# One-hot products for the last two experts, and a final LayerNorm that reads PSUM

## The reference

```
ffn = moe_ffn(x)                 # top 6 of 64 experts per token, each row weighted, summed per token,
                                 # plus one shared expert
x   = layer_norm(ALPHA * x + ffn, ln2_g, ln2_b)
```

## Time and profile before

| | |
|---|---|
| median of 3 runs | 1415.52 us (1412.44 to 1415.74) |
| the profiled execution's own time | 1414.83 us |
| its span, first to last instruction | 1412.7 us |
| last matmul ends (expert 63, down) | 1372.6 us |
| last scatter lands | 1381.7 us |
| last VectorE instruction ends | 1408.4 us |

### The profile page before, as it was taken

One profiled execution on the slowest core, in us unless ns is written; L12 is line 12 of the kernel. 1 busy time (PEld: TensorE's weight loads), 2 busy tenths in 40 slices (PEclk: granted clock), 3 DMA queues, 4 the chain that ended last, 5 costly groups with the idle time before them and its releaser, 6 DMA issues.

```text
span 1412.7 us, 23233 instructions
## 1 busy us (share of the span) xinstructions
PE 1287.0 (91%) x8205; PEld 743.2 (53%) x8206; DVE 447.3 (32%) x893; ACT 309.6 (22%) x825; POOL 283.4 (20%) x356
## 2 busy tenths in 40 slices
PE   8999999999999997999999999968797999988980
PEld 6465565556555445888846854534343444534430
DVE  1545544544441543333234711101111211111106
ACT  2232331333131343222223111101111011111110
POOL 2201110110110332000000132332223132342132
PEclk8999999999999998999999999988998999998995
DMA  4541111112300112333682189999999999999984
GB/s 123 165 126 39 45 52 52 52 45 81 119 1 0 45 45 68 90 93 85 232 349 87 42 325 392 396 387 401 401 408 390 407 388 375 371 382 395 405 294 182
DMA packets 126441, 294.35 MB, mean 208 GB/s; under 512 B 13008, under 2 KB 82768, under 8 KB 101664
## 3 DMA queue, kind: packets, MB, share of 16 engines
q1 hardware_dynamic: 108592, 265.66, 49.4%
q0 software_dynamic: 15632, 25.47, 7.6%
q10 hardware_dynamic: 2144, 2.22, 0.5%
HBM read 278.83 MB, written 27.04 MB: 217 GB/s over the span
## 4 chain that ended last, share of the span: by engine, by line
PE 34%; DMA 22%; DVE 3%; issue 1%; SPq 0%; ACT 0%; POOLq 0%; POOL 0%; DVEq 0%; ACTq 0%
DMA expert_gu<-in_expert_w_gate_up_dram 14%; PE bank L1227 11%; PE bank L1795 10%; PE bank L1802 5%; PE bank L1233 4%; DMA expert_down<-in_expert_w_down_dram 4%; DMA sum_rows<-expert_y,row_col 2%; PE bank L1787 1%; PE bank L1867 1%; DMA sum_rows<-over_y,over_row_col 1%; PE bank L1255 1%; PE bank L1846 1%; PE bank L1248 0%; DVE x_rows L2007 0%; DVE x_rows L2014 0%
## 5 line engine op out<-in xcount | busy, mean ns | idle before, releaser
L1795 PE MATMUL bank<-expert_gu,gathered_xT 128*64 128x256 f32 x2048 | 263.1, 411 | 52.5 <-DMA expert_gu<-in_expert_w_gate_up_dram 51.4
L442 PE MATMUL bank<-xT,w_head 128*128 128x512 f32 x480 | 241.0, 613 | 1.2 <-PEq L85 1.2
L1795 PEld LDWEIGHTS bank<-expert_gu,gathered_xT 128*64 128x64 f32 x2048 | 147.9, 142 | 148.8 <-DMA expert_gu<-in_expert_w_gate_up_dram 43.5
L1957 DVE SCALAR_TENSOR_TENSOR hidden<-gate,slot_w,bank 128x128 f32<-128x128 f32 x64 | 22.2, 347 | 436.4 <-ACT gate L1919 430.9
L1802 PE MATMUL bank<-expert_down,hiddenT 128*64 128x512 f32 x512 | 123.7, 603 | 1.6 <-issue 0.8
L1697 POOL DMA_INDIRECT sum_rows<-expert_y,row_col x64 | 101.2, 1581 | 49.4 <-POOL row_col L1692 47.9
L442 PEld LDWEIGHTS bank<-xT,w_head 128*128 128x128 f32 x480 | 78.8, 190 | 48.6 <-issue 42.5
L620 POOL TENSOR_TENSOR LO<-LT_diagonal,level_blocks 128x256 f32<-128x256 f32 x48 | 38.2, 830 | 233.5 <-DVE LT_corner L786 233.5
L1919 ACT ACTIVATE gate<-bank 128x128 f32<-128x128 f32 x64 | 17.8, 278 | 301.6 <-PE bank L1795 298.4
L1930 ACT COPY expert_y<-bank 128x512 f32<-128x512 f32 x63 | 36.9, 586 | 130.2 <-PE bank L1802 130.2
L1692 POOL COPY row_col<-row_idx 128x1 int32 (+1 forms) x64 | 12.5, 196 | 261.6 <-ACT expert_y L1930 166.7
(11 more groups left out here) (331 smaller groups left out, 1856.8 us busy)
## 6 DMA issues: line engine op xcount, KB each, us to landing
expert_gu<-in_expert_w_gate_up_dram SPq DMA_DIRECT2D x128, 1024.0 KB
expert_down<-in_expert_w_down_dram SPq DMA_DIRECT2D x64, 1024.0 KB
w_head<-in_w_in_dram SPq DMA_DIRECT2D x32, 512.0 KB, 3.9
w_tile<-in_w_in_dram SPq DMA_DIRECT2D x15, 512.0 KB, 4.2
sum_rows<-zero_rows SPq DMA_DIRECT2D x2, 2048.0 KB, 12.1
w_tile<-in_w_branch_a_dram SPq DMA_DIRECT2D x7, 512.0 KB, 5.4
w_pair<-in_w_in_dram SPq DMA_DIRECT2D x6, 512.0 KB, 5.2
x_rows<-in_x_dram SPq DMA_DIRECT2D x4, 512.0 KB
```

What stands on the lines that cost most here:

```text
L442: mm = nc.tensor.matmul(bank[:, :], w_head[:, g, c, :], xT[:, c, :], start=(c == 0), stop=(c == KC - 1))
L1795: mm = nc.tensor.matmul(bank[parts[a], 0:2 * P], x[:, c, part], halves[:, a, :, :], start=(c == 0), stop=(c == KC - 1))
```

## The change

The results of experts 62 and 63 are no longer scattered. For each of them a matrix of ones and zeros is built: partition r (a row of the block, for half a) has a one in column n where `row_idx` says that row r belongs to token n. POOL makes the row numbers 2n + a with two `iota` instructions of 64x512 ahead of its last turn, and DVE compares them with the two experts' `row_idx` in step 2 of the last turn (one small copy and two `tensor_scalar` of 128x512, ahead of that step's `copy_x`). After its last down products TensorE multiplies these matrices with `y`, 64 rows deep, into PSUM banks, and adds `odd_sums` and `xs` there by products with the identity. `xs` gets `even_sums` on DVE instead of on POOL. The statistics and the first of the two LayerNorm passes read PSUM, in halves of 512 columns. SP no longer waits for the scatters of experts 62 and 63. Piece t = 3 uses the banks of t = 0, and TensorE waits for them.

```diff
+    row_of = at("row_of", [P, SEQ], "w_t", 8192)
+    hot_row = at("hot_row", [P, DIRECT, SEQ], "w_t", 8192 + 4 * SEQ)
+    z_banks = [(ps[2], ps[3]), (ps[0], ps[1]), (ps[4], ps[6]), (ps[2], ps[3])]
 # sync; DIRECT = 2
         for k in (0, 2):
-            sp.wait_ge(scattered[k], 16 * NE // GROUP)
+            sp.wait_ge(scattered[k], 16 * (NE // GROUP - k // 2))
...
         for k in (1, 3):
-            sp.wait_ge(scattered[k], 16 * NE // GROUP)
+            sp.wait_ge(scattered[k], 16 * (NE // GROUP - k // 2))
 # gpsimd
-                if not (first and s == 0):
+                if not (first and s == 0) and not (last and s > STEPS - DIRECT):
                     scatter(i, s - 1, first and s < 3)
...
+        for a in range(2):
+            nc.gpsimd.iota(row_of[parts[a], :], pattern=[[2, SEQ]], base=a, channel_multiplier=0,
+                           allow_small_or_imprecise_dtypes=True).then_inc(rows_ready, 1)
+            pool.wait_ge(rows_ready, a + 1)
         turn(TURNS - 1, last=True)
         nc.gpsimd.memset(blank_word[:, 0:1], 0.0).then_inc(over_added, 1)
-        scatter(TURNS - 1, STEPS - 1, last=True)
...
-        pool.wait_ge(sd_done, 2 * TT)
-        for t in range(TT):
-            pool.wait_ge(sums_in[0][t], 16)
-            nc.gpsimd.tensor_tensor(xs[:, t, :], xs[:, t, :], even_sums[:, t, :], ALU.add).then_inc(even_added, 1)
 # tensor
+        def direct(t, n):
+            k, now = block_at(TURNS - 1, STEPS - DIRECT + n)
+            pe.wait_ge(y_ready[k], now)
+            for a in range(2):
+                nc.tensor.matmul(z_banks[t][a][:, :], hot_row[parts[a], n, t * P:(t + 1) * P], y[parts[a], k, :],
+                                 start=(n == 0), stop=False)
+        def sums_and_rest(t):
+            pe.wait_ge(sums_in[1][t], 16)
+            for a in range(2):
+                nc.tensor.matmul(z_banks[t][a][:, :], ident[:, :], odd_sums[:, t, a * HALF:(a + 1) * HALF], start=False, stop=False)
+            pe.wait_ge(even_added, t + 1)
+            for a in range(2):
+                mm = nc.tensor.matmul(z_banks[t][a][:, :], ident[:, :], xs[:, t, a * HALF:(a + 1) * HALF], start=False, stop=True)
+            mm.then_inc(z_psum, 1)
+        pe.wait_ge(hot_ready, 1)
+        for n in range(DIRECT):
+            for t in range(TT - 1):
+                direct(t, n)
+        for t in range(TT):
+            if t == TT - 1:
+                pe.wait_ge(ln_m, TT + 1)
+                for n in range(DIRECT):
+                    direct(t, n)
+            sums_and_rest(t)
 # vector, in the last turn's step 2
+                if last and s == 2:
+                    dve.wait_ge(rows_ready, 2)
+                    nc.vector.tensor_copy(hot_at[:, :], row_idx[:, NE - DIRECT:NE]).then_inc(rows_ready, 1)
+                    dve.wait_ge(rows_ready, 3)
+                    for n in range(DIRECT):
+                        mm = nc.vector.tensor_scalar(hot_row[:, n, :], row_of[:, :], hot_at[:, n:n + 1], None, ALU.is_equal)
+                    mm.then_inc(hot_ready, 1)
 # vector, at the end
         for t in range(TT):
-            dve.wait_ge(sums_in[1][t], 16)
-            dve.wait_ge(even_added, t + 1)
-            nc.vector.tensor_tensor(xs[:, t, :], xs[:, t, :], odd_sums[:, t, :], ALU.add).then_inc(odd_added, 1)
-            dve.wait_ge(odd_added, t + 1)
+            dve.wait_ge(sums_in[0][t], 16)
+            nc.vector.tensor_tensor(xs[:, t, :], xs[:, t, :], even_sums[:, t, :], ALU.add).then_inc(even_added, 1)
+        for t in range(TT):
+            dve.wait_ge(z_psum, t + 1)
             for half in range(2):
-                nc.vector.bn_stats(stats[:, t, half, :], xs[:, t, half * HALF:(half + 1) * HALF]).then_inc(st_done, 1)
+                nc.vector.bn_stats(stats[:, t, half, :], z_banks[t][half][:, :]).then_inc(st_done, 1)
...
-            nc.vector.scalar_tensor_tensor(out=xs[:, t, :], in0=xs[:, t, :], scalar=mv[:, t, 0:1], in1=g_row[:, :],
-                                           op0=ALU.subtract, op1=ALU.mult).then_inc(ln_m, 1)
+            for half in range(2):
+                of = slice(half * HALF, (half + 1) * HALF)
+                mm = nc.vector.scalar_tensor_tensor(out=xs[:, t, of], in0=z_banks[t][half][:, :], scalar=mv[:, t, 0:1],
+                                                    in1=g_row[:, of], op0=ALU.subtract, op1=ALU.mult)
+            mm.then_inc(ln_m, 1)
```

More of the change, by code:

```diff
@@ L1601, in experts_phase @@
     sums_in = [mem.sems(f"sums_in{n}_", TT) for n in range(2)]
-    even_added, odd_added = mem.sem("even_added"), mem.sem("odd_added")
+    even_added, z_psum = mem.sem("even_added"), mem.sem("z_psum")
+    rows_ready, hot_ready = mem.sem("rows_ready"), mem.sem("hot_ready")
     ln_in = mem.sem("fln_in")
@@ L1628, in experts_phase @@
     g_row, b_row = at("ln2_g_row", [P, D], "w_t"), at("ln2_b_row", [P, D], "w_t", 4096)
+    DIRECT = 2
+    row_of = at("row_of", [P, SEQ], "w_t", 8192)
+    hot_row = at("hot_row", [P, DIRECT, SEQ], "w_t", 8192 + 4 * SEQ)
+    hot_at = at("hot_at", [P, DIRECT], "w_t", 8192 + 4 * SEQ * (DIRECT + 1))
+    z_banks = [(ps[2], ps[3]), (ps[0], ps[1]), (ps[4], ps[6]), (ps[2], ps[3])]
     stats = at("ln2_stats", [P, TT, 2, 6], "qkT", 1664)
@@ L1680, in gather, with scatter @@
                 bounds_check=last_token, oob_is_err=False).then_inc(gathered[q], 16)
-        def scatter(i, s, alone=False, last=False):
+        def scatter(i, s, alone=False):
             k, now = block_at(i, s)
[L1685 to L1688, removed]
+            pool.wait_ge(y_ready[k], now)
             if not alone:
@@ L1694, in scatter @@
             pool.wait_ge(col2_ready[k], now)
-            if last:
-                pool.wait_ge(y_ready[k], now)
             nc.gpsimd.indirect_dma_start(
```

## The result

The changed kernel took 1407.1 us (median of 5 runs, 1405.17 to 1408.35), the kernel before 1415.5 beside it: ratio 0.994 [0.992, 0.996]. That lies in the predicted range, 1.9 us under the predicted 1409.0.

The account below looks back on a forecast made before the run. The end was bound by a chain of odd scatters and loads, then VectorE. First piece complete at 1385.8 plus 16.5 us of VectorE gives 1402.3 against 1408.4, 6.1 us less: 1409.0 us forecast, range 1405 to 1412.5.

Parts of the forecast that it names:

- Ahead of the end, cost 0: POOL's two iotas (at most 1.0 us each) and VectorE's copy and compares (under 2.2 us) fit in idle time.
- Even sums: SP's first even load goes out at 1371.6 instead of 1375.94, 4.3 us earlier.
- the rival of late odd sums: Loads beside scatter 61 stretch it to 9.69 us; odd piece 0 lands at 1383.1, total 1412; chance 0.12.
- Odd piece 0: First piece of the odd-sum loads lands at 1380.5, between 1379.9 and 1381.6.
- One-hot products: On TensorE after the down products, six pairs side by side at 0.86 us each, through at 1377.8; bounds 5.2 or 10.3 us.
- The identity products: TensorE, 3.42 us per piece; one clock fall after a 2.7 us pause costs 1.7 us (bounds 0, 2.5); chance 0.45.
- The 64-row products: Rival at TensorE's one-hot products: run one after the other they end at 1382.9, total 1411; chance 0.05.
- The clock stayed up: Rival: odd piece 0 a microsecond earlier, TensorE's pause 1.7 us, end 1400.6, 7.8 us less, total 1407.4; chance 0.30.
- stay at 0.5 through the identity products: Rival: TensorE at half clock, 6.83 us a piece, end 1415.6, 7.2 us more, total 1422; chance 0.05.
- VectorE per piece: VectorE's cycle in the end falls from 5.34 to 4.1 us, the last piece 4.2; bounds 4.05 to 4.4.
- The sum: Last VectorE instruction ends at 1402.3 against 1408.4, 6.1 us less; profiled execution 1408.7, forecast 1409.0.

Follow-up runs that it names:

- the moved-work kernel: Changed kernel with the identity products of xs for pieces 0 to 2 moved ahead of the wait for odd sums; 1409.9 us, ratio 0.9961 to the kernel before.
- the third trace: Changed kernel profiled and timed a third time, no new edit; 1409.8 us, ratio 0.9955 to the kernel before.
- The filler run: Changed kernel plus five identity products of y into a bank nobody reads, behind the one-hot products; 1410.0 us, ratio 0.9951 to the kernel before.
- sums in PSUM alone: Changed kernel without one-hot products, all 64 experts scattered, SP waiting for all; ratio 0.9991 to the kernel before.
- The orders that close the pause: Changed kernel with xs products of pieces 0 to 2, or only 0 and 1, ahead of the odd ones; ratios 0.9961 and 0.9901 to the kernel before.
- the last trace: Changed kernel with xs products of pieces 0 and 1 first, then odd ones piece by piece, run again; 1409.2 us, ratio 0.9941 to the kernel before.

## Why the prediction was right, and where it was not

**Ahead of the end, cost 0: right.** The two iotas took 1.79 us together, inside an idle stretch of POOL that left another 9.58 us unused behind them; the compares took 0.88, bounded at 2.2 with copy and waits, and VectorE was idle again before its next work.

**Even sums: right.** The first even load went out 1.5 us before the last down product's end, 1.0 was predicted. Scatter 61 took 4.68 us, as in the earlier trace rows, so the rival of late odd sums by a 9.69 us scatter didn't occur. The odd loads went out 1.2 us after the down products (1.4 predicted).

**Odd piece 0: the first mis-sized term.** Predicted at 7.9 us after the down products, between 5.3 and 7.0 us of stream, "closer to the clean figure because only scatter 61 is beside". Measured: 9.5, 9.8 and 8.2 in the three traces of this kernel. From the first even issue to this landing it was 11.0, 11.4 and 9.4 us, where 8.9 were reckoned. In the first trace the start-up explains it: the first even piece alone took 5.8 us, not 3.6. In the second it doesn't: that piece took 4.0 us, and the odd one was the latest of the three. The start-up of 3.6 us came from a trace in which scatter 63 ran beside the even loads, so a scatter beside them doesn't always slow them. Whether scatter 61 has a part in it the runs leave open: without it the odd piece landed 10.0 us behind the first even issue, inside the 9.4 to 11.4 with it.

**One-hot products: right.** Twenty-four records in 5.42 us, 5.2 predicted; the pairs run side by side. A mode change cost what the rows said: in the moved-work kernel the eight records of piece 3 occupied 1.92 us to the next start, 0.2 more than two pairs in a stream.

**The identity products: the second mis-sized term.** The prediction has one fall of the clock at 1.7 us after a pause of 2.7, with the row of the 2.5 us wait as its measure. That was the right mechanism and the right row: the third trace, with a pause of 2.86, lost 1.8 (5.4 us to z(0), where 3.6 are full clock). But with the piece late, the pause was 4.2 and 4.5, and the loss 3.1 and 2.9, more than the upper bound of 2.5 taken from the 4.38 us wait. The filler run isolates it: the same products from the same place after the down products, no pause, 3.6 us where 6.8 and 6.6 stood. That the loss grew because the pause did isn't shown: after 6.20 us (even loads waiting for the scatter) it was 2.1, after 13.46 us (sums in PSUM alone) 2.4. Over all pauses of 2.5 us and more it lies between 1.7 and 3.1, in no order of their length. The Trainium skill (TensorE: Matmul & The Clock Gate, HAM oscillation — how this bites in real kernels) says of another kernel that its products start cold behind each transfer wait, and advises a loop order that keeps TensorE busy. The orders that close the pause agree, with a clock of 1 where the changed kernel had 0.5. A wait as short as 1.21 us (the last trace) left it at 1.

**The other rivals.** The 64-row products did not run one after the other, as shown above. The clock stayed up only where products filled the pause, or all but 1.2 us of it. That rival's end is also misreckoned: it keeps the landing at 1380.5, though the rival has the piece land a microsecond earlier; with it the end is 1399.6, 8.8 us less and not 7.8. The clock did not stay at 0.5 through the identity products either: in all three traces it was back at 1 within the first piece (by 1384 in the first); later pieces follow without a wait. The case against this rival was put too strongly, though. In the trace of the kernel before, TensorE is busy without a pause from 15 to 25 us, and the clock is 0.50 all that time (thirty-two small products take 6.85 us, as slow as sixteen in 3.43). So it doesn't always come back after 3 to 6 us of work, and the last transfer wait had ended at 4.7 us, long before.

**VectorE per piece: nearly right.** (1396.82 - 1384.17) / 3 = 4.22 us a piece, 4.1 predicted. bn_stats from PSUM cost what it costs from SBUF (1.29 for two). The first LayerNorm pass, in halves from a bank, takes 1.41 us and 1.45 to the next start where 1.32 was put. Over four pieces, 0.4 us.

**The sum.** 29.7 + 1.6 (landing) + 1.5 (clock) + 0.4 (VectorE) = 33.2, the measured tail. In the third trace, with 8.2 and 2.86, it was 30.6. Against the two tails of before (35.8 and 36.7) that is a gain of 2.5 to 3.5 us where the first piece is late, and of 5.3 to 6.2 in the third trace. Another 0.4 us of the time lies outside the span, and the prediction took it as unchanged: the executions took 2.0 to 2.1 us more than their span in the two traces of before, 1.6 to 1.7 in all others. The three ratios, 0.994, 0.9969 and 0.9955, scatter around a gain of 6 us: the forecast of 6.1 is near their middle. But that the first comparison came so near to the forecast was in part luck. Three terms, 3.5 us together, went against the prediction, and more than half of that trace's difference lay ahead of the tail.

**Where the rest of the expected gain stays.** It turned into a wait and a slow stretch: 4.2 us in which TensorE stands idle for a transfer, and 3 us which that idleness costs afterwards. The order of TensorE's queue decides it. The odd sums, which come last, stand first in each group, ahead of `xs`, which is ready nearly 4 us earlier (1372.29 + 1.26 against 1377.39).

## What to carry to other kernels

When a change puts TensorE on the path of a tail that it had no part in, look for the pause ahead of its first product: queue what is ready earlier ahead of what lands last, and only as much as the wait holds, because more than that becomes the bound itself. Two edits that are each worth nothing can be worth 3 to 6 us together, when one brings the data early and the other shortens the engine that would eat the lead; a trial of one alone says little about the pair. And compare such a tail by its own ends in the traces: a difference of spans can come from a stretch in which both programs are the same.

## What the runs showed of the hardware

- Pauses of TensorE of 4.2 and 4.5 us cost 3 us behind them, where the products ran at half clock; one of 2.9 us cost 1.8, one of 6.2 us 2.1, one of 13.5 us 2.4; one of 1.2 us cost nothing. Products whose result nobody reads avoided the loss.
- The last down product ended between 1367.5 and 1375.0 over the fourteen traces. Most of that scatter arises at the very start, in instructions that all kernels share: the product of L205 started between 34.5 and 42.0, and from there it took 1331.5 to 1334.9 us. The small products at the start ran at half speed for a shorter or a longer time (sixteen in 1.86 or in 3.43 us). What sets that stayed open.
- Plain loads of 512 KB queued beside a scatter landed their first piece in 3.6 to 6.8 us, in the one trace without a scatter in 3.3. Whether the scatter has a part in the spread, and what else has, stayed open.
